# One layer of a four-mixer decoder on one core: token norm by blocks, four-quadrant small matmuls, gates multiplied in PSUM, exchanged down banks

## What is computed

```python
h = (_rms(x, norm1_g[l]) * valid).astype(dt)
z = h @ w_in[l]
# four mixers on slices of z: stick-breaking attention, retention, RWKV-7, sliding window
gates = jax.nn.sigmoid(gz.astype(jnp.float32)).reshape(B, L, N_BRANCH, D_MODEL)
merged = (gates[:, :, 0] * (y_sb.astype(dt) @ p_sb[l]) + gates[:, :, 1] * (y_ret.astype(dt) @ p_ret[l])
          + gates[:, :, 2] * (y_rw.astype(dt) @ p_rw[l]) + gates[:, :, 3] * (y_sw.astype(dt) @ p_sw[l]))
x = x + (merged.astype(dt) @ w_o[l]).astype(dt)
h2 = _rms(x, norm2_g[l]).astype(dt)
x = x + squared_relu_mlp(h2, w_up[l], w_down[l]).astype(dt)
```

## Time and profile before

| | us |
|---|---|
| median of three runs | 1309.74 (1306.81 to 1312.76) |
| profiled execution, its own time | 1307.6 |
| its span | 1305.8 |
| busy PE / weight loads | 1230.2 / 1014.9 |
| busy DVE / ACT / POOL | 464.8 / 487.2 / 467.0 |
| DMA moved | 110.17 MB |

### The profile page before, as it was taken

One profiled execution on the slowest core, in us unless ns is written; L12 is line 12 of the kernel. 1 busy time (PEld: TensorE's weight loads), 2 busy tenths in 40 slices (PEclk: granted clock), 3 DMA queues, 4 the chain that ended last, 5 costly groups with the idle time before them and its releaser, 6 DMA issues.

```text
span 1305.8 us, 21002 instructions
## 1 busy us (share of the span) xinstructions
PE 1230.2 (94%) x9042; PEld 1014.9 (78%) x9042; DVE 464.8 (36%) x834; ACT 487.2 (37%) x784; POOL 467.0 (36%) x287
## 2 busy tenths in 40 slices
PE   5999999989999999999899999889899999999998
PEld 4998877877789768767577777668788888788886
DVE  3599322323232262444263485362422100122000
ACT  6456312212222243677544635331543311233210
POOL 2443425143423223423331432233144544244541
PEclk9999989999999999999999999999899999999999
DMA  6222322113221113110511221142132333122330
GB/s 230 82 66 87 116 74 88 47 58 106 74 72 38 50 52 113 61 36 33 213 66 57 83 81 49 49 145 81 49 97 93 111 102 97 61 89 95 116 126 33
DMA packets 33340, 110.17 MB, mean 84 GB/s; under 512 B 4048, under 2 KB 6064, under 8 KB 32608
## 3 DMA queue, kind: packets, MB, share of 16 engines
q1 hardware_dynamic: 25952, 92.44, 21.5%
q10 hardware_dynamic: 6784, 16.26, 3.4%
q0 software_dynamic: 512, 0.13, 0.1%
HBM read 99.42 MB, written 9.04 MB: 83 GB/s over the span
## 4 chain that ended last, share of the span: by engine, by line
PE 77%; DVE 11%; ACT 6%; issue 2%; POOL 2%; DMA 2%; ACTq 0%; DVEq 0%; SPq 0%; POOLq 0%
PE pst L1623 17%; PE pst L1624 15%; PE pst L1625 15%; PE pst L1778 4%; PE pst L1777 4%; PE pst L1776 4%; PE pst L2076 2%; PE pst L2067 2%; DMA sw_v<-wait_sw_v 1%; ACT w_hi L784 1%; PE pst L1815 1%; PE pst L1802 1%; DVE merged L1309 1%; PE pst L2093 1%; PE pst L2051 1%
## 5 line engine op out<-in xcount | busy, mean ns | idle before, releaser
L667 POOL TENSOR_TENSOR w_lo<-raw,w_hi 128x1024 fp32r<-128x1024 f32 x164 | 401.2, 2452 | 714.9 <-ACT w_hi L784 703.3
L1623 PE MATMUL pst<-h_hi,w_hi 128*128 128x512 f32 (+1 forms) x960 | 357.7, 373 | 4.1 <-DVE x L1328 2.6
L1624 PE MATMUL pst<-h_lo,w_hi 128*128 128x512 f32 (+1 forms) x960 | 346.2, 361 | 0.0
L1625 PE MATMUL pst<-h_hi,w_lo 128*128 128x512 f32 (+1 forms) x960 | 346.0, 360 | 0.0
L784 ACT ACTIVATE w_hi<-raw 128x1024 fp32r<-128x1024 f32 x164 | 171.1, 1050 | 147.1 <-PE pst L1778 114.3
L1623 PEld LDWEIGHTS pst<-h_hi,w_hi 128*128 128x128 f32 x960 | 182.8, 190 | 40.6 <-issue 5.7
L1624 PEld LDWEIGHTS pst<-h_lo,w_hi 128*128 128x128 f32 x960 | 182.9, 190 | 27.4 <-issue 2.2
L1625 PEld LDWEIGHTS pst<-h_hi,w_lo 128*128 128x128 f32 x960 | 182.5, 190 | 27.7
L1623 PE MATMUL pst<-w_hi,h_hi 128*128 128x256 f32 (+3 forms) x328 | 94.2, 288 | 6.8 <-DVE h_lo L1495 3.7
L1778 PE MATMUL pst<-w_hi,u_lo 128*128 128x512 f32 x256 | 99.6, 389 | 0.0
L1777 PE MATMUL pst<-w_lo,u_hi 128*128 128x512 f32 x256 | 99.6, 389 | 0.0
(11 more groups left out here) (320 smaller groups left out, 1751.0 us busy)
## 6 DMA issues: line engine op xcount, KB each, us to landing
raw<-in_weights SPq DMA_DIRECT2D x164, 512.0 KB, 3.4
xt<-in_x SPq DMA_DIRECT2D x4, 512.0 KB, 5.4
wait_gate<-stage ACTq DMA_DIRECT2D x8, 256.0 KB, 2.0
gate_t<-wait_gate ACTq DMA_DIRECT2D x1, 2048.0 KB, 8.9
x<-in_x ACTq DMA_DIRECT2D x1, 2048.0 KB, 8.6
out<-x SPq DMA_DIRECT2D x8, 256.0 KB, 3.3
cst<-in_consts SPq DMA_DIRECT2D x1, 1524.0 KB, 10.4
wait_ret_v<-stage ACTq DMA_DIRECT2D x8, 128.0 KB, 1.9
```

The lines of the kernel that those rows point to most:

```text
L667: nc.gpsimd.tensor_tensor(w_lo[:, u % W_SLOTS, :], raw[:, u % RAW_SLOTS, :], w_hi[:, u % W_SLOTS, :].bitcast(F32), ALU.subtract).then_inc( ...
L1623: M(out, lh, rh, start=(first and i == 0), stop=False)
L1624: M(out, lh, rl, start=False, stop=False)
L1625: last = M(out, ll, rh, start=False, stop=(final and i == len(terms) - 1))
```

## The change

Seven things are changed; the dense work itself and the fill tables are the same.

1. **Start.** The gain row is broadcast once by two matmuls with a row of ones into banks 6 and 7; the norm on DVE multiplies each token row by its scale and by that gain at once. Blocks go one by one in the order 0, meta, 1, 2, 3, each with its own banks; the first half of the columns of the first dense job needs blocks 0, meta and 1 alone. Weight unit 0 is loaded behind token block 1, the tables behind units 1 and 2. The first two dense jobs run as four halves.
2. **Four quadrants.** Odd heads write the other half of the output rows and another bank (`turned`, `by_parity`, `places`). Each read of them by ACT or DVE becomes three instructions (one of 128 partitions for even heads, two of 64 for odd heads). The second copy behind F is split between ACT and DVE, and so is that behind WZ.
3. **Masks.** POOL makes `level_mask(b, 0)` and `level_mask(b, 1)` ahead of the low parts of the score piece.
4. **Gates in PSUM.** The gate product is written back into the job's PSUM bank, then added to `merged`; the bank is released after the addition.
5. **First s and early squares.** DVE's softplus is a step of its own, `sb_soft`; that of head 0 stands behind two dense jobs. ACT converts two more weight units before it waits in `sb_prep`. The first two `ret_square` stand ahead of the last piece of retention's block loop.
6. **Last norm.** DVE's part of `norm2_turn` becomes `norm2_low` and stands later; `up_early` computes the first 256 tokens of the first two up jobs, between the last turns.
7. **Down banks.** c = 1 uses 4 to 7; c = 0 uses 1, 3 and then the two banks of the up jobs, behind waits for their read-out at f = 0.

Also, SBUF places are rounded to 128 bytes, and `merged`'s split goes to `x_hi`, `x_lo` at the place of `h_hi`, `h_lo`.

```diff
+            def turned(b):
+                if b == 0:
+                    return [(slice(0, MB), slice(0, MB))]
+                return [(slice(CH * i, CH * i + CH), slice(CH - CH * i, P - CH * i)) for i in range(2)]
+            def by_parity(b, g):
+                h0, every = 4 * g, slice(0, rw_blocks[b][0])
+                return [(every, every, slice(h0, h0 + 4, 2), 4 + 2 * g)] + \
+                       [(to, at_, slice(h0 + 1, h0 + 4, 2), 5 + 2 * g) for to, at_ in turned(b)]
...
-                        for h in range(4 * g, 4 * g + 4):
-                            o = CH * (h % 4)
-                            for rows, _, _ in chunks:
-                                last = M(pst[rows, 4 + 2 * g, o:o + m], MM[rows, step % 2, h, 0:m],
-                                         TT[rows, h, 0:m], start=True, stop=True)
+                        for rows, out_rows, h in places(b, g):
+                            o = CH * (h % 4 // 2)
+                            last = M(pst[out_rows, 4 + 2 * g + h % 2, o:o + m], MM[rows, step % 2, h, 0:m],
+                                     TT[rows, h, 0:m], start=True, stop=True)
...
-                V.tensor_scalar(src, src, rs0[0:r, b:b + 1], None, ALU.mult).then_inc(hn_ready, 1)
+                V.scalar_tensor_tensor(out=halves(src), in0=halves(src), scalar=rs0[0:r, b:b + 1], in1=pst[0:r, 6:8, :],
+                                       op0=ALU.mult, op1=ALU.mult).then_inc(hn_ready, 1)
...
+            pe.wait_ge(turn_in, 16)
+            for b in (0, NB, 1):
+                token_turn(b)
+            feature_job(PHASE_C[0], ALL, 0, 2)
+            token_turn(2)
+            token_turn(3)
+            feature_job(PHASE_C[1], ALL, 0, 2)
+            feature_job(PHASE_C[0], ALL, 1, 2)
+            feature_job(PHASE_C[1], ALL, 1, 2)
...
-                        V.scalar_tensor_tensor(out=gtmp[:, b % 2, :], in0=gate_t[:, b, :], scalar=1.0, in1=one,
-                                               op0=ALU.add, op1=ALU.mult).then_inc(job_out[kind], 1)
-                        dve.wait_ge(job_out[kind], kind_no(n) + 1)
-                        V.tensor_tensor(merged[:, b, :], merged[:, b, :], gtmp[:, b % 2, :], ALU.add)\
-                            .then_inc(merged_ready, 1)
+                        link(V.scalar_tensor_tensor(out=one, in0=gate_t[:, b, :], scalar=1.0, in1=one,
+                                                    op0=ALU.add, op1=ALU.mult))
+                        V.tensor_tensor(merged[:, b, :], one, merged[:, b, :], ALU.add).then_inc(job_out[kind], 1)
...
             for b in range(NB):
                 jobs(1)
+                if b >= 2:
+                    g("norm2_low", b - 2)
                 g("norm2", b)
                 if b:
                     g("norm2_turn", b - 1)
+            g("up_early", 0)
+            g("norm2_low", NB - 2)
             g("norm2_turn", NB - 1)
+            g("up_early", 1)
+            g("norm2_low", NB - 1)
...
             def down_bank(c, blk):
-                return (4 if c == 0 else 0) + blk
+                if c == 1:
+                    return 4 + blk
+                s = job_slot(JOB_NO[("up", 0, FH - 1)])
+                return [1, 3, 2 - 2 * s, 2 * s][blk]
```

More of the change, by code:

```diff
@@ L299, in build @@
         top = SBUF_END - 4 * (2 * T + KD * T + KD * T + 2 * 4 * T)
-        at = [top]
-        gtmp = place("gtmp", [P, 2, T], at=at)
+        at = [top + 4 * 2 * T]
         gate_t = place("gate_t", [P, KD, T], at=at)
@@ L491, in halves, with h_bank, h_parts @@
             return row.rearrange("p (a b) -> p a b", a=2)
+        TOKEN_ORDER = [0, NB, 1, 2, 3]
+        def h_bank(b, half):
+            return [2, 4, 4, 6][b] + half
+        def h_parts(b):
+            if b == NB:
+                return [(pst[:, 1, 0:KD * MB].rearrange("p (k c) -> p k c", k=KD), (slice(0, KD), slice(0, MB)), 3)]
+            cols, n = slice(MB + P * b, MB + P * b + P), [1, 4, 6, 8][b]
+            return [(pst[:, h_bank(b, i), :].rearrange("p (k c) -> p k c", k=4), (slice(4 * i, 4 * i + 4), cols), n + i)
+                    for i in range(2)]
         def job_slot(n):
@@ L1539, in _ @@
                             dve.wait_ge(u_done[g], step - b)
-                            V.tensor_tensor(XX[0:n, hs, 0:m], XX[0:n, hs, 0:m],
-                                            four(pst[0:n, 5 + 2 * g, 0:256])[:, :, 0:m], ALU.add).then_inc(added, 1)
+                            for to, at_, hp, bank in by_parity(b, g):
+                                last = V.tensor_tensor(XX[to, hp, 0:m], XX[to, hp, 0:m],
+                                                       two(pst[at_, bank, 256:384])[:, :, 0:m], ALU.add)
+                            last.then_inc(added, 1)
                         if last_level:
@@ L2008, in sw_out, with up_early @@
                 last.then_inc(do_done, 1)
+            def up_early(i):
+                n = JOB_NO[("up", 0, i)]
+                s = job_begin(n)
+                pe.wait_ge(h2lo_ready, 2 * KD)
+                for k in range(KD):
+                    up_product(s, UNIT_NO[units_of(JOBS[n])[0]], k, slice(0, T // 2))
             def norm2_turn(b):
@@ L2082, in _ @@
                     pe.wait_ge(x_ready[g], level0[b] + levels_of[b])
-                    for h in range(4 * g, 4 * g + 4):
-                        for rows, _, _ in chunks:
-                            last = M(pst[rows, 4 + 2 * g, HD * (h % 4):HD * (h % 4) + HD], AM[rows, h, 0, 0:m],
-                                     VT[rows, HD * h:HD * h + HD], start=True, stop=True)
+                    for rows, out_rows, h in places(b, g):
+                        o = HD * (h % 4 // 2)
+                        last = M(pst[out_rows, 4 + 2 * g + h % 2, o:o + HD], AM[rows, h, 0, 0:m],
+                                 VT[rows, HD * h:HD * h + HD], start=True, stop=True)
                     last.then_inc(f_done, 1)
```

290 lines of the change are left out of this document (178 added, 112 removed).

## The result

The changed kernel takes 1258.22 us (median of four runs, 1257.34 to 1258.43) against 1310.03 before: a ratio of 0.9604, with a 95% interval of 0.9582 to 0.9627. The forecast was 1256, with a range of 1244 to 1280.

The account below looks back on a forecast made before the run. TensorE (PE), busy for 1230.2 of 1305.8 us, was taken as the bound. The terms summed to 56.0 us, less 3 as allowance; 1307.6 - 53 + 1 gave 1256 us, with a range of 1244 to 1280.

Parts of the forecast that it names:

- four quadrants: RWKV levels, C1 and update: 40 steps of 32 records fall from 1.08 to 0.6 us, saving 19.2 us.
- the last norm: Before the up projection: adding first and early half jobs cut PE's waits and slow clock, saving 7.1 us.
- the first s: Stick-breaking start: PE's wait for `sb_vm`, copied behind head 0's softplus, goes, saving 3.1 us.
- F and WZ: RWKV blocks, after the levels: halved matmuls and the extra reads cancel, 0 us, +0.6 to -0.5 for each of four blocks.
- The start: Kernel start: dense work begins near 13.8 instead of 24.07 us, behind fewer blocks and transposes, saving 8.1 us.
- the masks: RWKV block 2: PE's wait for `rw_m` behind POOL's low parts, and the slow clock after it, go, saving 6.0 us.
- the early squares: Retention: PE's wait for `ret_sq` goes, saving 2.6 us.
- the down banks: Down projection: PE's wait for DVE's additions to x, and the slow clock behind it, go, saving 4.4 us.
- Rival A: RWKV small matmuls don't get faster in the new layout: 1276 us, chance 0.12 for 1270 to 1280.
- Cover: RWKV levels: the three PSUM reads by DVE and ACT hide behind a dense piece of about 3 us.
- rival C: RWKV levels: reads crossing partition halves outrun the dense work; 1346 us at 1.0 us a read, chance 0.03.
- Gates: Last branch's merge: the gate product in PSUM shortens PE's waits for `gtmp` and `h_lo`, saving 5.5 us.

## Why the prediction was right

The total was off by 2 us, inside the range and near its likeliest value, and most of the mechanisms that it named are in the trace. That the number came out so near is in part luck. By the ledger four quadrants, the last norm, the first s and F and WZ with the short pieces fell short of their terms by 2.2, 4.3, 1.6 and 2.7, 10.8 in all. Against this stand the 3 set aside for such things and 3.8 at the up products that no term foresaw; the clock and the other terms come to the rest. Of the signs that it named, `sb_vm` was still waited for (1.6, not under 0.5), the clock still fell at the norm, and PE is busy for 1197.4, below the 1205. The faster up products (4.2) and the shorter F and WZ (0.46 and 0.86 a block, 5.3 in four) were not in the 1205.

**Right in mechanism and size.** The start (8.1 forecast, 8.7 measured), the masks (6.0 and 5.3), the early squares (2.6 and 2.9) and the down banks (4.4 and 4.5). The order of POOL at block 2, in its timeline, shows the masks' step as the prediction named it:

```profile
242.81 0.73 POOL L802 TENSOR_TENSOR rw_m<-rw_scores,cst 128x256 f32<-128x256 f32 x1 [25.13 <-DVE rw_scores L1607]
246.71 2.41 POOL L802 TENSOR_TENSOR rw_m<-rw_scores,cst 128x256 f32<-128x256 f32 x3 [3.16 <-DVE rw_scores L1607]
249.08 4.73 POOL L725 TENSOR_TENSOR w_lo<-raw,w_hi 128x1024 fp32r<-128x1024 f32 x2
```

The low parts follow the masks; the longest wait for `rw_m` fell from 4.3 to 0.4.

**Four quadrants.** The step "15.9 ns a record, with 0.1 for the turn" gave 0.60; measured 0.63, and 17.0 instead of 19.2, since of each block's first C1 only 0.2 is saved: its second group waits 0.4 for a mask. Even with the turns of shape inside, 0.63 over 32 records is 19.6 ns. The Trainium skill, in "TensorE: Matmul & The Clock Gate", Back-to-back issue gap, has about 25 ns as the least from start to start of small matmuls; by that rule (an estimate from that page) the steps would have been 0.8. The trace doesn't agree here either. Rival A is out.

**Cover, rival C.** A read across the halves costs no more than one inside. ACT's three copies of 128 elements for F in block 1, two of them across, took 0.84 us, 0.28 each, as the earlier trace rows had it:

```profile
225.22 0.84 ACT L1223 ACTIVATE rw_wz<-pst 128x128 f32<-128x128 f32 x3 [0.40 <-PE pst L2211]
```

In the levels PE waits 0.6 in all. The same rule of the page on tiling that stood with rival C (the Trainium skill, "TensorEngine Tiling (Array Packing)", PSUM Bottleneck) did hold at F and WZ, where nothing covers the reads.

**F and WZ, the step that failed.** I took 0 for it, within bounds of +0.6 to -0.5 for each block; it cost 0.5 a block. The row for WZ had the answer: 1.95 us from WZ's start to the first product before, in which the next group's matmuls hid the first group's copy. With matmuls at twice the rate and a copy of three reads nothing of that is left, and PE waits 1.09 and 0.98 where it waited 0.18.

**The last norm was mis-sized**, 7.1 for 2.8. I left 1.6 of waiting; there are 0.8 for `h2n`, 1.8 for `x_lo` (0.9 before the change, in `h_lo` at L1507) and 2.0 for `w_lo`. The first two are 1.0 more than I left; the third is a new wait. The rest of the missing 4.3 is in two steps of the working. The clock wasn't wholly won back, as a stretch of the changed kernel shows (length, busy of PE, PEld, DVE, ACT and POOL, granted clock, DMA):

```profile
898.00:902.00 4.00, 4.00 (x24) 4.00 (x24) 2.04 (x8) 0.88 (x4) 0.00 (x0) 0.62 0.01 4
```

And two halves cost more than the whole: 0.36 us for three matmuls of 256 columns, twice, against 0.68 for three of 512 at the full clock, 0.6 us over the two jobs. I had asked what the half jobs put in front of the last steps, and not what they take from behind the first job: 2.8 us of cover for the next weights.

**First s: half.** The wait for `sb_vm` shrank from 3.1 to 1.6. DVE's eight copies of the keys stand ahead, and one of them meets POOL's low part. The tile's summary (duration in ns, least, median, longest, and first and last start) before the change and after:

```profile
L1337 DVE COPY sb_kmd<-sb_k x8: 174/178/460, 487.8 to 489.6; 64x32 f32<-64x32 f32 x8
```

```profile
L1422 DVE COPY sb_kmd<-sb_k x8: 173/179/2275, 458.0 to 461.8; 64x32 f32<-64x32 f32 x8
```

**Gates: near in size (5.5 forecast, 5.1 measured), for a part of the reason.** I priced the two waits at 7.7 and left 2 for the series at the branch's end (which gives 5.7, where the sum has 5.5). The series cost 1.8 (`x_lo`), but the later release of the bank, which I held free, cost 2.1 once, because a split of 2.47 stood ahead of the product, and 0.2 twice more; at the projection of the branch before, the same wait took 0.7 in two places, which stands in the row of the sliding window. So the waits of the last branch gave 3.3. Most of the rest is clock that I hadn't priced: behind the waits for `h_lo` the kernel before ran at half speed, which the changed kernel doesn't do there. The kernel before:

```profile
884.00:888.00 4.00, 2.84 (x13) 2.85 (x14) 1.11 (x2) 1.32 (x2) 2.37 (x1) 0.59 0.00 0
```

Undoing the edit alone costs 7.0, more than the 5.1 by which before and after differ; the longer waits (5.0 and 3.7 against 4.0 and 3.7) and the clock behind them make up the difference, and why POOL is met once more was not looked into.

**Missing: the rows.** The tiles were noted in the change and not costed. The trace of before had both rates: the down products, over weights whose pieces begin 2048 bytes apart, at 227 ns, and the up products at 232 ns. 4.2 us were there to be read.

**The clock.** Between 168 and 186 us the clock falls to its lower level, 1.2 GHz, in every version of the changed kernel, behind RWKV block 0's light steps. How long it stays differs. The same two stretches (us, length, busy and instructions of PE, PEld, DVE, ACT, POOL, granted clock, DMA share, GB/s) in the changed kernel and in the one with rows of 2176 bytes, which is the same up to there:

```profile
176.00:180.00 4.00, 3.13 (x33) 2.75 (x35) 1.38 (x2) 1.19 (x2) 0.00 (x0) 0.66 0.02 8
180.00:184.00 4.00, 4.00 (x55) 3.03 (x48) 1.29 (x2) 0.00 (x0) 0.74 (x1) 1.00 0.01 2
```

```profile
176.00:180.00 4.00, 3.44 (x16) 3.04 (x15) 1.21 (x2) 1.20 (x2) 0.00 (x0) 0.50 0.00 0
180.00:184.00 4.00, 3.68 (x36) 3.09 (x37) 1.46 (x3) 0.00 (x0) 0.30 (x1) 0.50 0.01 2
```

That is 2 us between one kernel and the next, with no cause in their work. Against the kernel before, the changed kernel won 1.5 there. In the sliding window part it lost 1.5 near 708 us, and won 1.5 back near 800, where the kernel before (near 830 in its own time) had its slow stretch.

## What to carry to other kernels

Small products that use half of the array are worth spreading over all four quadrants, as long as dense work covers the extra reads; where nothing covers them, one read and slower matmuls is faster. When a job is cut in two to fill a gap, look at what was hidden behind the whole job, its successor's weights first. An instruction of DVE with two SBUF operands should not stand ahead of the instruction that frees a bank while POOL is at work, and the distance of rows and the place of a moving operand are worth a look at the time from matmul to matmul.

## What the runs showed of the hardware

- Records of 64x64 products in two quadrants start every 34 to 35 ns in the mean, in four quadrants every 20, and it matters little whether neighbours alternate or come in runs of four (21 ns).
- Reads of PSUM that go from one half of the partitions to the other take 0.28 us for 128 elements, no more than others.
- Matmuls of 512 columns over a moving operand with rows 2176 bytes apart start every 232 ns, over rows 2048 or 2304 bytes apart every 227 ns (the tiles `x_hi`, `x_lo`). With tiles on multiples of 32 bytes in place of 128 the products over `x_hi` stayed at 227, and those over `y_hi`, with rows of 2048, went from 227 to 233.
- A copy of 32 elements on DVE from SBUF to SBUF took 2.28 us in place of 0.18 beside POOL's work.
- The time at the lower clock behind the same light stretch differs from kernel to kernel with the same work there: between 180 and 184 us one was granted 1.00 and one 0.50, 2 us of difference.
